# First stage of a decoder step on one core: the first weight piece and thirteen constant columns loaded first, the second piece split ahead of the squares, and GpSimd adding the squares for a single product

## The reference, cut to what matters

```python
def rmsnorm(x, g):
    xf = x.astype(jnp.float32)
    y = xf * lax.rsqrt(jnp.mean(xf * xf, axis=-1, keepdims=True) + RMS_EPS)
    return (y * g.astype(jnp.float32)).astype(x.dtype)

def a_qkv(x, pos, norm_g, w_qkv, qn, kn):
    n, t, _ = x.shape
    qkv = (rmsnorm(x, norm_g) @ w_qkv).reshape(n, t, 3, N_HEADS_A, HEAD_DIM)
    q = rope(rmsnorm(qkv[:, :, 0], qn), pos)
    k = rope(rmsnorm(qkv[:, :, 1], kn), pos)
    return q, k, qkv[:, :, 2]
```

## Time and profile before

| what | us |
|---|---|
| median of three runs (lowest, highest) | 1786.38 (1779.15, 1789.33) |
| the profiled execution | 1783.73 |
| its span | 1782.0 |
| TensorE busy | 1669.5 (94%) |
| VectorE busy | 1339.1 (75%) |
| ScalarE busy | 1032.0 (58%) |
| GpSimd busy | 76.3 (4%) |

### The profile page before, as it was taken

The page is one execution under the profiler, slowest core; times in us unless marked ns, Lnnn a source line. Parts: engine busy times, 40 slices in busy tenths (PEclk is TensorE's granted clock), DMA queues, the critical chain, the costliest instruction groups (busy, mean ns, idle before and its releaser), DMA issues.

```text
span 1782.0 us, 25119 instructions
## 1 busy us (share of the span) xinstructions
PE 1669.5 (94%) x9238; PEld 1382.0 (78%) x9238; DVE 1339.1 (75%) x1540; ACT 1032.0 (58%) x995; POOL 76.3 (4%) x121
## 2 busy tenths in 40 slices
PE   7997889999989788499999999999999999999998
PEld 6884569999978556388888888878878878878886
DVE  5873346665577553888898898898888888988987
ACT  5443344433444232467767777777767777777775
POOL 0003210000000210100000000000000000000000
PEclk9997789999999777699999999999999999999999
DMA  9346424444653420199999999999999999999995
GB/s 331 110 148 205 131 79 153 158 139 130 202 175 113 163 72 25 59 321 342 363 338 343 353 338 341 358 338 345 354 344 343 351 332 360 343 329 371 335 344 199
DMA packets 233622, 453.50 MB, mean 254 GB/s; under 512 B 8224, under 2 KB 80032, under 8 KB 233296
## 3 DMA queue, kind: packets, MB, share of 16 engines
q1 hardware_dynamic: 224656, 421.82, 67.6%
q0 software_dynamic: 8896, 30.74, 5.3%
HBM read 447.81 MB, written 4.72 MB: 254 GB/s over the span
## 4 chain that ended last, share of the span: by engine, by line
PE 85%; DVE 6%; ACT 3%; issue 2%; DMA 2%; POOLq 0%; POOL 0%; DVEq 0%; SPq 0%; ACTq 0%
PE psum L279 24%; PE psum L281 23%; PE psum L280 23%; PE psum L783 1%; PE psum L818 1%; PE psum L593 1%; DVE wlo L275 1%; PE psum L798 1%; PE psum L569 1%; PE psum L582 1%; ACT whi L271 1%; DVE rs L1187 1%; PE psum L568 1%; PE psum L523 1%; PE psum L634 1%
## 5 line engine op out<-in xcount | busy, mean ns | idle before, releaser
L275 DVE TENSOR_TENSOR wlo<-raw,whi 128x2048 fp32r<-128x2048 f32 (+1 forms) x404 | 911.9, 2262 | 208.1 <-ACT whi L271 207.7
L271 ACT ACTIVATE whi<-raw 128x2048 fp32r<-128x2048 f32 (+1 forms) x404 | 764.9, 1896 | 304.3 <-PE psum L281 303.3
L279 PE MATMUL psum<-whi,xgh 128*128 128x512 f32 x896 | 360.7, 403 | 8.5 <-DVE wlo L275 7.1
L280 PE MATMUL psum<-wlo,xgh 128*128 128x512 f32 x896 | 356.0, 397 | 0.0
L281 PE MATMUL psum<-whi,xgl 128*128 128x512 f32 x896 | 355.6, 397 | 0.0
L279 PE MATMUL psum<-hh,whi 128*128 128x288 f32 x800 | 246.4, 308 | 12.9 <-DVE hl L1320 8.5
L281 PE MATMUL psum<-hh,wlo 128*128 128x288 f32 x800 | 240.4, 300 | 0.0
L280 PE MATMUL psum<-hl,whi 128*128 128x288 f32 x800 | 239.8, 300 | 0.0
L279 PEld LDWEIGHTS psum<-whi,xgh 128*128 128x128 f32 x896 | 169.4, 189 | 50.9 <-DVE wlo L275 10.6
L281 PEld LDWEIGHTS psum<-whi,xgl 128*128 128x128 f32 x896 | 169.4, 189 | 41.1
L280 PEld LDWEIGHTS psum<-wlo,xgh 128*128 128x128 f32 x896 | 169.6, 189 | 38.6
(11 more groups left out here) (299 smaller groups left out, 1669.8 us busy)
## 6 DMA issues: line engine op xcount, KB each, us to landing
raw<-in_w_gu_moe SPq DMA_DIRECT2D x226, 1024.0 KB, 5.2
raw<-in_w_down_moe SPq DMA_DIRECT2D x112, 1024.0 KB, 5.0
raw<-in_w_gu_dense SPq DMA_DIRECT2D x22, 1024.0 KB, 5.1
raw<-in_w_qkv_a SPq DMA_DIRECT2D x12, 1024.0 KB, 12.7
raw<-in_w_down_dense SPq DMA_DIRECT2D x16, 704.0 KB, 4.6
kraw_a<-in_cache_a_k POOLq DMA_DIRECT2D x32, 256.0 KB, 3.3
vraw_a<-in_cache_a_v POOLq DMA_DIRECT2D x32, 256.0 KB, 3.3
raw<-in_w_q_b SPq DMA_DIRECT2D x6, 1024.0 KB, 5.2
```

What stands on the lines that cost most here:

```text
L271: nc.scalar.activation(whi[:, p % SPL, 0:size], raw[:, p % RAW, 0:size], ACT.Copy).then_inc(hi_ready, 1)
L275: nc.vector.tensor_tensor(wlo[:, p % SPL, 0:size], raw[:, p % RAW, 0:size], whi[:, p % SPL, 0:size].bitcast(F32), ALU.subtract).then_inc(p ...
L279: nc.tensor.matmul(out, lh, rh, start=start, stop=False)
L280: nc.tensor.matmul(out, lh, rl, start=False, stop=False)
```

## The change

1. **Constants.** The 13 columns that the start needs (`g_attn_a`, four head gains, `eps`) are moved to the front of the constant array and loaded first, by a load of their own (semaphore `gains_loaded`); the other columns come in a second load, behind piece 1.
2. **Order of SyncE's loads.** Gains, piece 0, xT, piece 1, the rest of the constants, pieces 2 to 5, mask, piece 6 and on.
3. **Order on ScalarE.** A Sqrt of a one-column tile `warm` comes first; then the split of piece 0, the eight `hh`, the split of piece 1, the eight squares, the root.
4. **Order on VectorE.** The low part of piece 0 comes first; then `hn` and `hl` by turns, then the low part of piece 1, a wait for the rest of the constants, the reciprocal.
5. **The sum of squares.** GpSimd makes seven adds, behind its first six key pages; TensorE makes one product with `featsum` behind tile 1 of the projection, in place of eight products ahead of it, and waits for the rest of the constants only there.

```diff
-for _name, _n in (("ident", P), ... ("over", 2 * NE * 2),
-                  ("g_attn_a", KD), ("g_ffn0", KD), ("g_kv", KD), ("g_attn_b", KD), ("g_ffn1", KD),
-                  ("qn_a", 1), ("kn_a", 1), ("qn_b", 1), ("kn_b", 1), ("eps", 1)):
+for _name, _n in (("g_attn_a", KD), ("qn_a", 1), ("kn_a", 1), ("qn_b", 1), ("kn_b", 1), ("eps", 1),
+                  ("ident", P), ... ("over", 2 * NE * 2),
+                  ("g_ffn0", KD), ("g_kv", KD), ("g_attn_b", KD), ("g_ffn1", KD)):
...
+NFIRST = KD + 5
...
+        warm = sb("warm", [P, 2])
...
         @block.sync
         def _(eng):
-            eng.dma_start(cst[:, :], io["const"]).then_inc(sem("const_loaded"), 16)
+            eng.dma_start(cst[:, 0:NFIRST], io["const"][:, 0:NFIRST]).then_inc(sem("gains_loaded"), 16)
+            load_piece(eng, 0, 0, W[0])
             eng.dma_start(xT[:, :, :], io["xT"]).then_inc(sem("x_loaded"), 16)
-            for p in range(RAW):
+            load_piece(eng, 0, 1, W[1])
+            eng.dma_start(cst[:, NFIRST:NCONST], io["const"][:, NFIRST:NCONST]).then_inc(sem("const_loaded"), 16)
+            for p in range(2, RAW):
                 load_piece(eng, 0, p, W[p])
...
             for n in range(A["kring"]):
                 key_page(A, n)
-            store(A, io["ak"], io["av"])
-            caches(A, A["kring"])
-
             def norm_add(tag, before):
...
-            norm_add("norm_f", 0)
-            norm_add("norm_b", KD - 1)
+            norm_add("norm_a", 0)
+            store(A, io["ak"], io["av"])
+            caches(A, A["kring"])
+
+            norm_add("norm_f", KD - 1)
+            norm_add("norm_b", 2 * KD - 2)
...
         @block.tensor
         def _(eng):
-            eng.wait_ge(sem("const_loaded"), 16)
...
                         ins.then_inc(tile_sem(tiles, m), 1)
+                        if m == 1 and b is A:
+                            eng.wait_ge(sem("const_loaded"), 16)
+                            norm_total("norm_a", KD - 1)
...
-            for k in range(KD):
-                norm_sum("norm_a", k)
             project(A, tiles_a, lambda m: ("norm_a", hh, hl))
...
         @block.scalar
         def _(eng):
-            eng.wait_ge(sem("const_loaded"), 16)
+            eng.wait_ge(sem("q_gains"), 1)
+            nc.scalar.activation(warm[:, 1:2], warm[:, 0:1], ACT.Sqrt)
+            eng.wait_ge(sem("gains_loaded"), 16)
...
-            eng.wait_ge(sem("x_loaded"), 16)
-            eng.wait_ge(sem("q_gains"), 1)
+            split_upto(0)
+            eng.wait_ge(sem("q_gains"), 2)
+            for k in range(KD):
+                norm_hi("norm_a", k, hh)
+            split_upto(1)
             for k in range(KD):
                 square("norm_a", k)
-                norm_hi("norm_a", k, hh)
-            split_upto(1)
             norm_root("norm_a")
...
         @block.vector
         def _(eng):
-            eng.wait_ge(sem("const_loaded"), 16)
+            nc.vector.memset(warm[:, :], 1.0).then_inc(sem("q_gains"), 1)
+            eng.wait_ge(sem("gains_loaded"), 16)
...
-            eng.wait_ge(sem("x_loaded"), 16)
-            for k in range(KD):
-                norm_gain("norm_a", "g_attn_a", k)
-            for k in range(KD):
-                norm_lo("norm_a", k, hh, hl)
+            split_upto(0)
+            for k in range(KD + 1):
+                if k == 0:
+                    eng.wait_ge(sem("x_loaded"), 16)
+                if k < KD:
+                    norm_gain("norm_a", "g_attn_a", k)
+                if k >= 1:
+                    norm_lo("norm_a", k - 1, hh, hl)
             split_upto(1)
+            eng.wait_ge(sem("const_loaded"), 16)
             norm_factor("norm_a")
             project(A, tiles_a)
```

More of the change, by code:

```diff
@@ L62 @@
 _at = 0
-for _name, _n in (("ident", P), ("headsum", 32), ("headspread", P), ("featsum", P), ("rot", P), ("cos", T), ("sin", T), ("before", P),
+for _name, _n in (("g_attn_a", KD), ("qn_a", 1), ("kn_a", 1), ("qn_b", 1), ("kn_b", 1), ("eps", 1),
+                  ("ident", P), ("headsum", 32), ("headspread", P), ("featsum", P), ("rot", P), ("cos", T), ("sin", T), ("before", P),
                   ("ones", P), ("slots", P), ("expert", NE * 3), ("over", 2 * NE * 2),
-                  ("g_attn_a", KD), ("g_ffn0", KD), ("g_kv", KD), ("g_attn_b", KD), ("g_ffn1", KD),
-                  ("qn_a", 1), ("kn_a", 1), ("qn_b", 1), ("kn_b", 1), ("eps", 1)):
+                  ("g_ffn0", KD), ("g_kv", KD), ("g_attn_b", KD), ("g_ffn1", KD)):
     CONST[_name] = (_at, _at + _n)
@@ L505, in project @@
                         ins.then_inc(tile_sem(tiles, m), 1)
+                        if m == 1 and b is A:
+                            eng.wait_ge(sem("const_loaded"), 16)
+                            norm_total("norm_a", KD - 1)
                         if m == 0 and b is B:
-                            norm_total("norm_b", 2 * KD - 2)
+                            norm_total("norm_b", 3 * KD - 3)
                     if m % 4 == 0 and 1 <= m // 4 <= nrot // 4:
@@ L719, in _ @@
                         if i == 0 and part == 0 and s == 0:
-                            norm_total("norm_f", KD - 1)
+                            norm_total("norm_f", 2 * KD - 2)
             for m in range(KD):
```

## The result

| what | before | after |
|---|---|---|
| median (lowest, highest) of 17 executions each, us | 1783.87 (1779.15, 1790.27) | 1792.84 (1787.66, 1799.3) |
| ratio, 95% interval | | 1.0052, 1.0038 to 1.0066 |
| the profiled execution | 1783.73 | 1787.66 |
| its span | 1782.0 | 1786.0 |

The change makes the kernel slower by 0.52%, 9.3 us by the ratio, with 6.8 to 11.8 as the interval. The profiled execution of after is the fastest of its 17, so the spans differ by 4.0 us only.

What follows compares the result with a forecast made beforehand. The first stage was taken as paced by ScalarE's split of piece 3, moved from 28.93 to 33.9 us by waiting for GpSimd's adds; other edits nothing. Median 1786.38 + 5.0 = 1791.4 us, range 1782 to 1798.

Steps and rivals of the forecast that it cites:

- The bound: First stage: paced by when ScalarE splits piece 3, at 28.93 us before, not by when TensorE starts its first tile.
- Loads: Start of the kernel: gains land at about 3 us, piece 0 at about 6.2, xT at about 9.15.
- Rival B: First loads: the small load holds the queue, piece 0 lands at 10.0 us; together +8.8, 1795 us; chance 0.1.
- The work ahead of the squares: Pieces 0 and 1: TensorE starts at about 11.75 us, 7.7 earlier; the eighth square is done at 20.2.
- GpSimd's adds: Sum of squares: first add held by VectorE until 19.8 us, ends 20.6; six more at 0.95 end at 26.3.
- rival C: GpSimd's first add takes no turns with VectorE: +3.6 us, 1790 us; chance 0.2.
- Behind the adds: Product at 26.45 us, reciprocal 27.67, tile 0 normed 31.87, split of piece 3 at 33.9 against 28.93.
- the sum's 5.0: Split of piece 3, and with it the kernel's end, comes 5.0 us later than before.
- its last step: After the split of piece 3: engines stand to each other as before, so the end shifts by 5.0 us.
- The whole: Total time: median 1786.38 us plus 5.0 gives 1791.4 us.
- Rival A: Projection: TensorE is the bound and its lead counts; 0.4 to 2.7 us less, 1785 us; chance 0.15.
- The edits that I had put at nothing: Start: products taken off TensorE, table loads, key pages, constants' second load and TensorE's dropped first wait change nothing.

Runs made afterwards that it cites:

- b_split_late: Kernel before, with eight useless squares ahead of ScalarE's split of piece 3: first transpose to tokens behind the projection at 125.7 us, against 121.6 before.
- a_late_pe: Changed kernel, with TensorE waiting for the input's last low part before its first tile: first transpose to tokens behind the projection at 126.8 us, against 128.4.
- a_split2: Changed kernel, with piece 2 split ahead of root and reciprocal: first transpose to tokens behind the projection at 127.0 us, against 128.4.
- the repeat: Changed kernel, unchanged, profiled a second time: first transpose to tokens behind the projection at 128.3 us, against 128.4 in the first profile.
- sum_between: Changed kernel, with TensorE's norm products between tile 0's matmuls, their matrix in the first load, no GpSimd adds: first transpose to tokens behind the projection at 121.3 us.

## Why the prediction was right, and where it was off

- **The bound.** The first stage is paced by the split of piece 3: right. T follows that split by 92.7 us in seven of the fourteen runs and by up to 1.7 more in the others but one, a delay put there alone passes through (b_split_late), and a later start of TensorE costs nothing (a_late_pe).
- **Loads.** The gains landed at 2.6 (3 forecast), piece 0 at 6.6 (6.2). Rival B, late first loads, is out: it needed piece 0 past 7.7.
- **The work ahead of the squares.** First matmul at 12.4 (11.75), squares done at 20.7 (20.2): late by 0.6 and 0.5, of which piece 0's landing makes 0.4.
- **GpSimd's adds.** First add 2.17 us (about 2.2), the last ends at 26.24 (26.3). The second figure owes something to luck: the first add ended 0.4 late (21.04 for 20.6), and a pace of 0.87 instead of 0.95 over six adds made 0.5 of that good. The turns between GpSimd and VectorE hold, and rival C is out. By the Trainium skill's rule (GPSIMD Engine Reference, 1. Specifications) a VectorE instruction with two SBUF inputs contends with GpSimd; the traces agree: an add takes 0.79 us alone and 2.17 beside one, and in a_split2 two take 3.59.
- **Behind the adds.** Split of piece 3 at 34.5 (33.9). In a_late_pe, with the clock up, it is 34.0, 5.1 us later than before: the sum's 5.0.
- **What the sum left out** is in its last step, "From there PE, VectorE and ScalarE stand to each other as before ..., the rows repeat, and the end shifts by 5.0". They didn't stand as before: the working had TensorE waiting 3 to 6 us ahead of the product (5.5 measured) and again for the turn, and I had read in the earlier trace rows the low clock behind a shorter wait, but put no price on it. It is 0.5 us at the root (27.7 in after, 27.2 in a_late_pe, the product taking 1.30 or 0.72) and 1.2 on the interval from split to T (93.9 against 92.7; 1.0 in the repeat): 1.7 together, so the end of the projection moved by 6.8, not 5.0. That these 1.7 are the clock's rests on a_late_pe, where both dips and the 1.6 go together, and on the table of steps above.
- **The whole.** 1791.4 forecast, 1792.84 measured. That is closer than the mechanism deserves: the median that I started from was 2.5 us above that of 17 executions. The shift itself is 9.3 us by the ratio against 5.0. 6.8 are shown; it is the lower end of the interval, and whether the other 2.5 are scatter of the attention stages or something that the change does there stays open. The chance of 0.15 for slower by over 0.5% was low for what came out at 0.52%.
- **Rival A**, TensorE's lead, was worth less than nothing. The edits that I had put at nothing came to nothing together up to T for the loads, the order and the table loads, as sum_between shows. The products taken off TensorE did not win time; kept there, inside tile 0 or behind tile 1, they beat the adds by 7.2 and 4.1 us at T.

## What to carry to other kernels

An engine that starts earlier gains nothing if what follows is held by another engine's list, as here. Find the instruction whose time the rest of the stage follows at a constant distance, and ask of every edit what it does to that one. A sum moved to GpSimd to spare TensorE can put an idle engine's work on the one path that counts, here 7.4 us of adds in place of 4.0 of products, and here it waited for VectorE's instructions as well. Look at the granted clock behind TensorE's pauses too: a dip cost up to 1.7 us here, or nothing, depending on where it fell.

## What the runs showed that I had not expected

- Starting TensorE 4.4 us later made the projection end 1.6 us earlier (a_late_pe). With the first pause cut from 5.5 to 1.0 us both dips of the clock were gone, although later pauses of 3.1 and 2.6 us stayed.
- Matmuls of no use in the pauses removed the two dips, and another stood elsewhere (0.59 from 34 to 38 us).
- One stage of the unchanged program took 94 or 100 us, at granted clocks of 0.78 and 0.71. The spread of the whole program's time, 11 us in either kernel's 17 executions, is larger but of that order.
